# The latent mixer with six weight units in place of twelve, queries made further ahead, and a new order inside each pair of heads

## The reference, cut to what matters

```python
def mla_mixer(x, w_dqkv, q_norm_g, w_uq, kv_norm_g, w_ukv, w_out, cos_m, sin_m):
    cq, ckv, k_rope = jnp.split(x @ w_dqkv, [Q_LORA, Q_LORA + KV_LORA], axis=-1)      # 384, 256, 32
    q = (rms_norm(cq, q_norm_g) @ w_uq).reshape(B, S, MLA_HEADS, MLA_NOPE + MLA_ROPE)  # 16 heads of 96
    q_nope, q_rope = q[..., :MLA_NOPE], apply_rope(q[..., MLA_NOPE:], cos_m, sin_m)
    kv = (rms_norm(ckv, kv_norm_g) @ w_ukv).reshape(B, S, MLA_HEADS, MLA_NOPE + MLA_V) # 64 + 64
    k_nope, v = kv[..., :MLA_NOPE], kv[..., MLA_NOPE:]
    k_rope = apply_rope(k_rope[:, :, None, :], cos_m, sin_m)
    q = jnp.concatenate([q_nope, q_rope], axis=-1)
    k = jnp.concatenate([k_nope, jnp.broadcast_to(k_rope, (B, S, MLA_HEADS, MLA_ROPE))], axis=-1)
    o = causal_block_attention(q, k, v, (MLA_NOPE + MLA_ROPE) ** -0.5)
    return o.reshape(B, S, MLA_HEADS * MLA_V) @ w_out
```

## Time and profile before

| | us |
|---|---|
| median of 3 runs (lowest, highest) | 2527.92 (2527.87, 2528.9) |
| the profiled execution | 2527.56 |
| its span | 2525.8 |
| PE busy (98% of the span) | 2463.6 |
| DVE busy (60%) | 1505.4 |
| ACT busy (47%) | 1184.3 |
| POOL busy (16%) | 399.0 |

### The profile page before, as it was taken

One profiled execution on the slowest core, in us unless ns is written; L12 is line 12 of the kernel. 1 busy time (PEld: TensorE's weight loads), 2 busy tenths in 40 slices (PEclk: granted clock), 3 DMA queues, 4 the chain that ended last, 5 costly groups with the idle time before them and its releaser, 6 DMA issues.

```text
span 2525.8 us, 32691 instructions
## 1 busy us (share of the span) xinstructions
PE 2463.6 (98%) x13213; PEld 2073.0 (82%) x13213; DVE 1505.4 (60%) x2146; ACT 1184.3 (47%) x1488; POOL 399.0 (16%) x463
## 2 busy tenths in 40 slices
PE   8999999999999999999989999999999999899999
PEld 6888878888888788888877888888878877898998
DVE  5546664464455645645566446446766567897644
ACT  5544554444444544444465444444554446444442
POOL 0002310000001100000131000001239802570000
PEclk9999999999999999999999999999999999999999
DMA  8554445555654455555334555555435543336553
GB/s 245 183 185 154 145 139 184 186 180 184 187 164 134 134 184 191 176 184 190 118 123 148 185 187 178 185 186 161 141 126 192 186 148 101 117 118 200 172 193 127
DMA packets 315542, 418.09 MB, mean 166 GB/s; under 512 B 18825, under 2 KB 273154, under 8 KB 315394
## 3 DMA queue, kind: packets, MB, share of 16 engines
q1 hardware_dynamic: 315394, 416.01, 51.2%
HBM read 414.92 MB, written 1.05 MB: 165 GB/s over the span
## 4 chain that ended last, share of the span: by engine, by line
PE 86%; DVE 6%; ACT 3%; issue 3%; POOL 1%; DMA 1%; SPq 0%; DVEq 0%; POOLq 0%; ACTq 0%
PE ps L597 25%; PE ps L599 24%; PE ps L598 24%; DVE wlo L469 2%; PE ps L614 2%; PE ps L2007 2%; PE ps L615 2%; PE ps L619 2%; PE ps L2264 1%; ACT whi L461 1%; PE ps L2313 1%; PE ps L2298 1%; PE ps L2253 1%; PE ps L1966 1%; DMA raw<-in_ffn_w_dram 1%
## 5 line engine op out<-in xcount | busy, mean ns | idle before, releaser
L469 DVE TENSOR_TENSOR wlo<-raw,whi 128x2048 fp32r<-128x2048 f32 (+1 forms) x397 | 909.5, 2296 | 608.3 <-ACT whi L461 607.5
L461 ACT ACTIVATE whi<-raw 128x2048 fp32r<-128x2048 f32 (+4 forms) x401 | 746.6, 1867 | 467.0 <-DMA raw<-in_ffn_w_dram 405.6
L597 PE MATMUL ps<-whi,xh 128*128 128x512 f32 (+3 forms) x1853 | 695.0, 375 | 8.5 <-DVE wlo L1386 2.5
L599 PE MATMUL ps<-whi,xl 128*128 128x512 f32 (+3 forms) x1853 | 687.7, 371 | 0.0
L598 PE MATMUL ps<-wlo,xh 128*128 128x512 f32 (+3 forms) x1853 | 687.3, 371 | 0.0
L597 PEld LDWEIGHTS ps<-whi,xh 128*128 128x128 f32 x1853 | 350.9, 189 | 73.7 <-issue 8.5
L599 PEld LDWEIGHTS ps<-whi,xl 128*128 128x128 f32 x1853 | 350.5, 189 | 60.0
L598 PEld LDWEIGHTS ps<-wlo,xh 128*128 128x128 f32 x1853 | 350.8, 189 | 57.8
L597 PE MATMUL ps<-whi,oh 128*128 128x512 f32 x944 | 380.0, 403 | 0.0
L599 PE MATMUL ps<-whi,ol 128*128 128x512 f32 x944 | 369.1, 391 | 0.0
L598 PE MATMUL ps<-wlo,oh 128*128 128x512 f32 x944 | 367.9, 390 | 0.0
(11 more groups left out here) (339 smaller groups left out, 2658.7 us busy)
## 6 DMA issues: line engine op xcount, KB each, us to landing
raw<-in_ffn_w_dram SPq DMA_DIRECT2D x352, 512.0 KB, 4.8
raw<-in_ffn_w_dram SPq DMA_DIRECT2D x88, 1024.0 KB, 4.9
raw<-in_w_ff_dram SPq DMA_DIRECT2D x32, 1024.0 KB, 5.3
raw<-in_w_out_dram SPq DMA_DIRECT2D x20, 1024.0 KB, 4.9
raw<-in_w_in_dram SPq DMA_DIRECT2D x20, 1024.0 KB, 5.1
raw<-in_dsa_w_in_dram SPq DMA_DIRECT2D x32, 512.0 KB, 4.8
raw<-in_dsa_w_in_dram SPq DMA_DIRECT2D x12, 1024.0 KB, 5.1
raw<-in_fox_w_in_dram SPq DMA_DIRECT2D x16, 512.0 KB, 4.6
```

The costliest lines, as they stand in the source:

```text
L461: act.activation(hi(u)[:, 0:w], raw[:, (slot[u] + 1) % SLOTS, 0:w], ACT.Copy).then_inc(sem("hi_ready"), 1)
L469: dve.tensor_tensor(lo(u)[:, 0:w], raw[:, (slot[u] + 1) % SLOTS, 0:w], hi(u)[:, 0:w].bitcast(F32), ALU.subtract).then_inc(sem("lo_ready"), 1)
L597: pe.matmul(o, ah, bh, start=start, stop=False, skip_group_check=True)
L599: return pe.matmul(o, al, bh, start=False, stop=stop, skip_group_check=True)
```

## The change

The four query units stay; the eight key and value units become two of 2 x 1024 columns, one for two quads. The order in memory is query 0, query 1, keys and values of quads 0 and 1, query 2, keys and values of quads 2 and 3, query 3. So 12 units become 6, and every later unit number is lower by 6. The queries of quad 1 get the banks 4 and 3 and are made before the attention begins; quad 1's keys and values too; quads 2 and 3 are made in pairs 0 to 5. The probabilities of pair i are turned ahead of the scores of pair i+1 (except pair 3). The orders of DVE, ACT and POOL inside a pair change with it.

The core of the diff (PE's latent_q and latent_kv get the matching waits and are left out):

```diff
+            units = NG + NQ2
-                for i in range(NG):
-                    if i == 0:
-                        out_.append(uq[:, :, 0:384])
-                    out_ += [ukv[:, :, 512 * i:512 * i + 256], ukv[:, :, 512 * i + 256:512 * i + 512]]
-                    if i < NG - 1:
-                        out_.append(uq[:, :, 384 * i + 384:384 * i + 768])
+                q = [uq[:, :, 384 * i:384 * i + 384] for i in range(NG)]
+                out_ = [q[0], q[1], ukv[:, :, 0:1024], q[2], ukv[:, :, 1024:2048], q[3]]
 # what attn_ahead gives for pair i (the unit split in it)
-                last = u + 3 * q + 4 + i % 2 + (i == 3)
+                return u + (5, 6, 7, 8, 8, 8, 9, 9)[i]
 # POOL
                     turn(0)
+                    if mla:
+                        turn(1)
 # ACT, pair i
+                        if mla:
+                            if i:
+                                outp(i - 1)
+                                split_hi(act, attn_ahead(st, i))
+                            if i in (1, 3, 4, 5):
+                                latents(*((2, 1), (2, 2), (3, 1), (3, 2))[(1, 3, 4, 5).index(i)])
+                            if i == 0:
+                                latents(2, 0)
+                            turned_p(i)
+                            if i + 1 < NP:
+                                exps(2 * i + 2)
+                                exps(2 * i + 3)
+                            if i == 0:
+                                split_hi(act, attn_ahead(st, 0))
+                            if i == 2:
+                                latents(3, 0)
 # DVE, latent stage, moved(t): between the copies of the turned latents and their low part
+                        if t:
+                            quad_lo(dve, st["end"] + 2, 0)
+                        else:
+                            split_lo_half(dve, st["end"] + 1, 0)
 # DVE, pair i
+                    for i in range(NP if mla else 0):
+                        for n in turns_at(st, i):
+                            turned_qk(n)
+                        recip(2 * i)
+                        recip(2 * i + 1)
+                        if i == 0:
+                            split_lo_half(dve, u + 4, 1)
+                        elif i < 6:
+                            split_lo(dve, attn_ahead(st, i))
+                        if i:
+                            low(i - 1)
+                        if i in (3, 4, 5):
+                            latent_values(*((2, 2), (3, 1), (3, 2))[i - 3])
+                        if i == 3:
+                            front(8)
+                        turned_p(i)
+                        if i + 1 < NP:
+                            if i != 3:
+                                front(2 * i + 2)
+                            front(2 * i + 3)
+                        if i == 0:
+                            split_lo(dve, attn_ahead(st, 0))
 ...
 # PE, before the pairs
                         latent_q(0, 0)
+                        latent_q(1, 0)
 ...
                         latent_kv(0, 1, [0])
+                        latent_kv(0, 2, [0])
                         pe.wait_ge(sem("la_ch"), 2)
                         latent_q(0, 1)
                         latent_kv(0, 1, [1])
-                        latent_kv(0, 2)
+                        latent_kv(0, 2, [1])
+                        latent_q(1, 1)
+                        latent_kv(1, 1)
                         pe.wait_ge(sem("la_krope"), 2)
-                        latent_q(1, 0)
-                        latent_q(1, 1)
                         turn(0)
+                        latent_kv(1, 2)
                         scores(0)
 # PE, in the pairs: after turn(i + 1)
+                            if i == 1:
+                                latent_kv(2, 1)
+                                pturn(1)
+                                scores(2)
+                            if i == 2:
+                                latent_q(3, 0)
+                                latent_q(3, 1)
+                                pturn(2)
+                                scores(3)
+                            if i == 3:
+                                latent_kv(2, 2)
+                                scores(4)
+                                pturn(3)
+                                pe.wait_ge(sem("qk_moved"), b("qk_moved", 0) + copied(3, 0))
+                                residual(pe, b("cx_ready"), 0)
```

209 lines of the change are left out of this document (140 added, 69 removed).

## The result

The changed kernel takes 2552.0 us (median of 4 runs, 2550.1 to 2552.8), the kernel before 2527.9 in the runs beside it: ratio 1.0093, 95% interval 1.008 to 1.0105, slower. I had said slower, 2540.5 with a range up to 2548: the direction was right and the size too small by 11.5 us. The profiled spans are 2548.3 and 2525.8 us, 22.5 apart; the forecast had 12.6 for that difference.

The account below looks back on a forecast made before the run. It took PE, busy 2463.6 of 2525.8 us, to bound the kernel. To 2527.56 us it added 1 for the mixer's stage and 11.6 for layer 3's ring, giving 2540.2 and a median of 2540.5, range 2528 to 2548.

Parts of the forecast that it names:

- PE's idle in the mixer's stage: Latent stage and pairs: 2 us idle in the latent stage, some 3, 2 and 4.4 in pairs 1, 2 and 3.
- low clock in the stage: Mixer's stage: PE at the lower clock behind new idle times costs 2 us, bounds 0 and 6.2.
- idle in layer 3: Turned slot ring delays the ffn's first two units: PE waits of 3.3 and 6.3 us, 9.6 in all.
- low clock in layer 3: Behind layer 3's two idle times a low clock costs 2 us, bounds 0 and 3.4.
- the clock's term: Low clock behind new PE idle, taken as 2 us in the mixer's stage and 2 us in layer 3.
- the latent stage's wait: PE's first key and value matmuls wait for DVE's half of the new unit: 2 us, bounds 0 and 2.3.
- the chain: Pairs with a 2048 column split: ACT and DVE in series, values 6.1 us after the exponential, next chain after 8.7.
- Values of pair 0: Mixer: the values of pair 0 start at about 1280.3, for 1279.55 before.
- From pair 0 to pair 3: Mixer: values of pair 0 to values of pair 3 take 28.6 us, for 25.4 before.
- From pair 3 to pair 7: Mixer: values of pair 3 to the last pair's take 31.2 us, for 36.0 before; PE's own work sets the pace.
- Worse: Rival: low clock at both its bounds and the latent stage's new wait grows; 2547 us, chance 0.12.
- The larger units: Eight 256 KB units become two of 1024 KB; the skill's rule gives 12.6 us of landing time, the sum took nothing.

Follow-up runs that it names:

- run 9: Run 2's kernel with DVE's splits cut in halves and put in DVE's pauses and behind the masks; 2525.3 us, ratio 0.9982 to the kernel before.
- run 10: Run 9's kernel with DVE's first half of the key and value unit's low part made earlier in the latent stage; 2525.4 us, ratio 0.9983.
- run 2: Changed kernel with the weight slots first handed out as 1, 2, 3, 4, 0, so layer 3's oproj has slots 1 to 4 again; 2535.3 us, ratio 1.0028.
- run 4: Run 2's kernel with DVE's low parts of weight splits moved behind its copies of turned probabilities and its masks; 2528.6 us, ratio 0.9998.
- run 3: Run 2's kernel with DVE waiting for POOL's scaling of both heads before it starts its split, order kept; 2532.2 us, ratio 1.0015.
- run 1: Kernel before with only the first order of the weight slots turned (4, 0, 1, 2, 3), as layer 3 has it in the changed kernel; 2542.8 us, ratio 1.0054.
- run 11: Run 9's kernel with ACT's split of oproj's third unit behind pair 3's exponentials and DVE's halves of it in pair 4; 2522.2 us, ratio 0.9973.
- run 6: Run 2's kernel with two units' low parts made from one SBUF input instead of two, so left out of the result; 2533.8 us, ratio 1.0019.
- run 7: As run 6, with output and input cut into unequal rows (3 x 682 and 2 x 1023 columns); 2537.4 us, ratio 1.0032.
- run 8: Run 4's kernel plus unused one-input DVE statistics in pairs 0 and 1, where the changed kernel has its split; 2529.7 us, ratio 1.0005.

## Why the prediction was wrong

The profiled executions lie 22.5 us apart where the forecast had 12.6. Here are the terms, in us. PE's work in the mixer's stage at the full clock is taken from run 9's trace (76.2); the forecast's idle there is its 92.3 us less that work and 2 of clock.

| term | forecast | changed kernel |
|---|---|---|
| PE's idle in the mixer's stage | 14.1 | 16.7 |
| low clock in the stage | 2 | 6.3 |
| idle in layer 3 | 9.6 | 8.8 |
| low clock in layer 3 | 2 | 5.1 |
| elsewhere | 0 | 0.8 |

**The step that failed** is the clock's term, twice "2 us": "In pair 1 a low clock lies beside the chain and costs little, behind pair 3 it falls on PE's own work. I take 2 us (bounds 0 and, for two falls like the one seen, 6.2)", and the same 2 us (bounds 0 and 3.4) in layer 3. The two were 11.4 us in place of 4, 7.4 of the 9.9 us missed between the traces, and each lies above its bound. There were four falls in the stage, not two: behind the latent stage's wait, in pair 0, in pair 1 and behind pair 3, 17 us at the lower clock in all, for 6.8 before. And the one in pair 1 didn't lie beside the chain. The scores of pair 2, from which DVE's mask and ACT's exponentials go on, took 2.77 us at the lower clock for 1.48 in the next pair: PE is a link of that chain. PE in the changed kernel, 1294 to 1306 us:

```profile
1294.88 2.77 PE L2381 MATMUL ps<-qkT 96*128 96x128 f32 x8
...
1303.71 1.48 PE L2381 MATMUL ps<-qkT 96*128 96x128 f32 x8
```

Whether a wait as short as the latent stage's brings a fall differs from execution to execution (run 10), so a part of the 6.3 is this execution's; run 2, the same mixer, has 4.5.

**The second step that failed** is the chain, which I wrote over ACT and DVE, with POOL's scaling inside it at its free price. PE's two waits in pair 1:

```profile
1291.24 0.52 PE L2417 MATMUL ps<-ident,pr 128*128 128x128 f32 x3 [2.87 <-POOL pr L863]
1294.21 0.87 PE L2417 MATMUL ps<-ident,pr 128*128 128x128 f32 x3 [2.46 <-POOL pr L863]
```

- *Values of pair 0.* I had them at 1280.3, 24.2 us into the stage. In run 9, with no collision and no low clock, they come after 24.5. In the changed kernel they come after 28.5: 1.0 us is POOL kept out by DVE's half split (a wait of 1.39 us for 0.41), 3.0 the low clock.
- *From pair 0 to pair 3* I had "28.6 us", and it took 31.3. PE's work at the full clock was forecast right (19.2 us; 19.1 in run 9). Its idle was 10.3 us for 9.4: in pair 1 2.87 + 2.46 = 5.3 for 3, since POOL waits behind the split of query unit 3 and then for the end of the 2048 column split; in pair 2 1.0 for 2, in pair 3 4.0 for 4.4. The other 2 us are the clock. The idle that I had named as a sign for pair 1, ended by DVE's copy of probabilities, isn't there; it is ended by POOL.
- *From pair 3 to pair 7* it took 32.8 us, for 31.2. PE's work was right again, 30.3 us (run 9 has 30.3). The rest is 1.3 us of idle for 0.9, and 1.2 of clock. That runs 4 and 9 take 32.8 us as well is chance: they have no low clock there and 2.5 us of idle.
- *What the collision is worth.* In idle leaving POOL out is 1.0 us ahead of pair 0's values and 2.3 in pair 1, of which 1.4 came back in pairs 2 and 3. But waits bring the clock down too, and run 3 puts the collision at 3 to 4 us of the total.
- *What held.* The chain of a pair whose scaling meets no split: in pair 3 from the exponentials' end (1308.5) to the values 7.8 us, for 8.1. The latent stage's wait: 1.87 for 2.

**Layer 3** was right in place, cause and idle (9.4 us in run 1, 8.8 in the changed kernel, for 9.6) and short by the clock: 4.7 and 5.1 for 2. In run 1 9.4 us of idle brought 4.7 us of clock behind it, half as much again.

**The rivals.** The result lies beyond the last one, *Worse* (2547, chance 0.12), which had the clock at both its bounds. Its second condition didn't come: the latent stage's wait was 1.87 us for 2. The stage's upper bound was added up wrongly by 0.2 (-0.9 + 6.2 is 5.3, not 5.5), which changes nothing.

**The larger units.** No wait of PE in the mixer ends by a DMA after the change either. One wait of ACT does: 0.93 us for the first key and value unit, until 1254.73. It isn't on the path, since ACT's part of the split ended at 1255.8 and DVE took the unit up at 1259.77. So the rule of the Trainium skill that the prediction weighed ("DMA: Bandwidth & Descriptors", "Rules for kernel authors", few large transfers for many small ones) brought as little here as I had said. With DVE's splits put elsewhere the same units and the same order of PE are faster than the kernel before, by 3.9 us (run 9) and 6.5 (run 11) by the medians on their chips. So the order had something to give, and the splits' place, the collision and the ring more than took it. How much of it better places for the splits would have given the kernel before, no run shows.

The sum: clock 7.4 us more than forecast, idle in the mixer 2.6 more and in layer 3 0.8 less, elsewhere 0.8, and 1.6 by which the changed kernel's median is further above its profiled execution than that of before. These add up to 11.6, for the 11.5 missed. The split into idle and clock in the mixer rests on one trace with no low clock. Open: what decides whether the clock falls behind a wait under 2.3 us, and whether run 11 is faster than run 9.

## What to carry to other kernels

When a chain is written out for the price of a new order, write in every engine that it passes, the nearly idle one too, and look in the trace at what runs on its neighbour in just that moment: POOL was busy a third of the time, and 8.7 us of PE's waits ended with it. A long operation on VectorE belongs in the time in which that engine waits anyway, and cut in two if the pause is short. When a ring of slots changes its length or its count, follow which unit falls on which slot to the end of the program; one line that turned it was worth 14 us. A pause of TensorE can cost more than its length: in layer 3 half as much again, and in the mixer every wait of 2.3 us and more had a fall of the clock behind it, shorter ones in some executions only. So count the pauses of a new order and price a fall behind each long one, and ask whether TensorE's own work in the low stretch is a link of the chain.

## What the hardware showed

VectorE and GpSimd hold each other up for whole instructions, in some pairs of operations and not in others. GpSimd's scaling of 128 columns (0.40 us alone, both inputs in SBUF) took 2.45, until 0.26 us behind the end of a split with two inputs from SBUF. It took 1.38 and 1.45 beside operations with one input on 2048 and 2046 columns (1.61 us, and 1.21, twice the pace of the split; runs 6 and 7). Beside statistics with one input, 512 columns in 0.6 us, it took 0.40 (run 8). The other way round an operation of VectorE on 2 columns took 0.55 us, until GpSimd was done (run 7). A copy from PSUM beside GpSimd's rotation slowed neither (0.56 and 1.70 us, run 4). The Trainium skill, "SBUF — State Buffer", section "SBUF: two separate sides", describes an exclusive lock: an operation of VectorE that works in a mode with two ports, or reads two inputs from SBUF while GpSimd's reads SBUF too, and one of GpSimd, hold the shared pair of ports for the whole instruction, whoever comes first. The first four cases agree with it, if the doubled pace of runs 6 and 7 is such a mode; that it is the ports and nothing else no run here shows.
